# First projections of an RG-LRU layer in blocks 1 to 9: strip pairs by seven block products on half of the contraction

## The reference

```python
u = rms_norm(x, g_pre[0])
proj = u @ w_in                       # 2048 x 5120
xr, gate = proj[..., :2560], proj[..., 2560:]
xc = conv_b + sum(xpad[:, k:k + T] * conv_w[k] for k in range(4))
r = sigmoid(blockwise(xc) @ w_r + b_r); i = sigmoid(blockwise(xc) @ w_i + b_i)   # 10 blocks of 256
a = exp(-8 * r * softplus(-lam)); b = sqrt(1 - a * a) * (i * xc)
h_t = a_t * h_(t-1) + b_t
y = h * silu(gate);  out = y @ w_out
```

## Time and profile before

| | us |
|---|---|
| three runs | 1775.84, 1776.43, 1777.09; median 1776.43 |
| profiled execution | 1776.33 |
| its span, first to last instruction | 1774.6 |
| mean granted clock of TensorE | 0.990 |
| TensorE busy | 1726.0 |
| VectorE, ScalarE, GpSimd busy | 1063.4, 880.8, 234.5 |

### The profile page before, as it was taken

How to read it: one execution, slowest core, us unless ns; L and a number is a source line. 1 busy time by engine, 2 the same in 40 slices (tenths; PEclk the granted TensorE clock), 3 DMA queues, 4 the chain that set the end, 5 groups by cost and what they waited for, 6 DMA issues and landing times.

```text
span 1774.6 us, 35741 instructions
## 1 busy us (share of the span) xinstructions
PE 1726.0 (97%) x14123; PEld 1673.3 (94%) x14123; DVE 1063.4 (60%) x1781; ACT 880.8 (50%) x1385; POOL 234.5 (13%) x182
## 2 busy tenths in 40 slices
PE   8999999999999999999999999999999999899997
PEld 7999999999999999999999999999998899799995
DVE  5676555675557632358856576665665666722365
ACT  6344443344434422345566666666675666622344
POOL 2000000000000011003132222322321121001110
PEclk9999999999999999999999999999999999999997
DMA  9232223323222232665522222222224787522565
GB/s 280 87 96 81 84 84 92 97 72 94 83 84 82 75 89 80 182 175 149 187 85 61 84 61 72 73 72 60 85 60 132 228 250 234 159 84 83 153 173 185
DMA packets 311715, 205.97 MB, mean 116 GB/s; under 512 B 9041, under 2 KB 287713, under 8 KB 311521
## 3 DMA queue, kind: packets, MB, share of 16 engines
q1 hardware_dynamic: 308668, 194.86, 37.6%
q0 software_dynamic: 2864, 9.15, 1.5%
q10 hardware_dynamic: 68, 0.41, 0.1%
HBM read 188.42 MB, written 15.97 MB: 115 GB/s over the span
## 4 chain that ended last, share of the span: by engine, by line
PE 42%; DVE 5%; issue 2%; ACT 1%; DMA 1%; SPq 0%; ACTq 0%; DVEq 0%
PE PS L799 11%; PE PS L801 11%; PE PS L800 10%; PE Z L1133 2%; DVE T L2198 1%; PE Z L1143 1%; PE Z L1167 1%; PE Z L1039 1%; PE Z L1070 1%; PE Z L1317 1%; PE Z L1036 1%; PE Z L1048 1%; PE Z L1037 1%; PE Z L1072 1%; PE Z L1071 1%
## 5 line engine op out<-in xcount | busy, mean ns | idle before, releaser
L799 PE MATMUL PS<-U,WS 128*128 128x272 f32 x3680 | 1082.2, 294 | 14.6 <-issue 3.4
L801 PE MATMUL PS<-U,WS 128*128 128x272 f32 x3680 | 1067.0, 290 | 0.0
L800 PE MATMUL PS<-U,WS 128*128 128x272 f32 x3680 | 1062.7, 289 | 0.0
L799 PEld LDWEIGHTS PS<-U,WS 128*128 128x128 f32 x3680 | 696.1, 189 | 21.3 <-issue 10.2
L800 PEld LDWEIGHTS PS<-U,WS 128*128 128x128 f32 x3680 | 696.4, 189 | 1.9
L801 PEld LDWEIGHTS PS<-U,WS 128*128 128x128 f32 x3680 | 695.0, 189 | 0.0
L1864 DVE TENSOR_TENSOR WS<-raw,WS 128x1024 fp32r<-128x1024 f32 (+1 forms) x202 | 256.7, 1271 | 314.8 <-ACT WS L1346 311.8
L1346 ACT ACTIVATE WS<-raw 128x1024 fp32r<-128x1024 f32 (+1 forms) x204 | 211.5, 1037 | 460.5 <-PE PS L801 460.4
L681 POOL TENSOR_TENSOR raw<-raw,GN 128x1024 f32<-128x1024 f32 x76 | 150.2, 1976 | 522.0 <-DMA raw<-in_b_w_in_dram 448.6
L703 POOL COPY T<-T 128x544 f32<-128x544 f32 x2 | 1.7, 864 | 609.9 <-ACT T L1491 561.2
L2210 DVE TENSOR_TENSOR T<-T,Z 128x256 f32<-128x256 f32 (+1 forms) x64 | 33.2, 519 | 62.0 <-PE Z L1049 61.4
(11 more groups left out here) (298 smaller groups left out, 2156.7 us busy)
## 6 DMA issues: line engine op xcount, KB each, us to landing
raw<-in_a_w_in_dram SPq DMA_DIRECT2D x80, 512.0 KB, 3.9
raw<-in_b_w_in_dram SPq DMA_DIRECT2D x64, 512.0 KB, 4.0
raw<-in_a_w_out_dram SPq DMA_DIRECT2D x32, 512.0 KB, 3.9
KPG<-in_cache_k_dram SPq DMA_DIRECT2D x64, 256.0 KB, 3.0
raw<-in_b_w_out_dram SPq DMA_DIRECT2D x32, 512.0 KB, 4.0
VPG<-in_cache_v_dram SPq DMA_DIRECT2D x60, 256.0 KB, 3.3
T<-scratch_x SPq DMA_DIRECT2D x64, 136.0 KB, 3.5
RAW<-in_a_w_out_dram SPq DMA_DIRECT2D x12, 512.0 KB, 4.4
```

What stands on the lines that cost most here:

```text
L799: pe.matmul(psum, w_hi, x_hi, start=first, stop=False)
L800: pe.matmul(psum, w_hi, x_lo, start=False, stop=False)
L801: return pe.matmul(psum, w_lo, x_hi, start=False, stop=last)
```

## The change

In blocks 1 to 9 two strips of a kind (branch, q = 0; gate, q = 1) are now made as one pair p = 2(i - 1) + q. For K tiles 8 to 15 nothing changes but the order (`straight`, 96 matmuls). On K tiles 0 to 7 the pair is a product of 2 x 2 blocks: two strips by two groups of four K tiles (`KQ`), and these by two halves of the tokens. It is made with seven block products of 12 matmuls instead of eight, in the form of Winograd. They are numbered 1 to 7 here in the order of TensorE's queue (`two_strips`).

For that there are four sums of weight blocks per pair, made by GpSimd (`SUMS`), each with a high part by ScalarE (`sum_high`) and a low part by VectorE (`sum_low`), and four sums of token blocks, made once, in block 0, by VectorE (`token_difference`), each again with two parts (`XT` and slots of `U`). The x tiles 0 to 7 are loaded back for it (`XX`) and scaled by ScalarE. A running sum in one bank (`A_BANK`) is copied at three points by ScalarE (`keep`, into `SNAP`), and VectorE adds the copies to the other banks when strips are evicted.

Further: the first tap of the convolution and the squares of the decay go from VectorE to ScalarE (`conv_tap`, `chain_square`); only the K tiles 4 to 7 of unit m + 1 need parts of their own (`second_weights`); the gate products use other banks (`gate_bank`); Y keeps 4 tiles, is stored to DRAM per block (`y_store`) and read back in the last one (`y_back`), since the sums need its place; the block loops are unrolled on all engines; two memsets of GpSimd move behind the stage. The second load of a slot (units m + 2 and m + 3) waits for GpSimd's sums (`w_sum`), GpSimd for the first two loads and the low part of the fourth sum before.

TensorE (the order of products and waits), from the diff:

```diff
+            def two_strips(i, q):
+                m, p = pair(i, q)
+                pe.wait_ge(w_low, m + 1)
+                if q:
+                    pe.wait_ge(snap, 3 * p)
+                else:
+                    pe.wait_ge(gates_out, 4 if i == 1 else 4 * i - 2)
+                product(A_BANK, w_of(0, 0), x_of(0, 0), True, False, p_done)
...
+                product(c_bank(q, 0, 0), w_of(0, KQ), x_of(KQ, 0), True, False, unit_done)
+                pe.wait_ge(s_low, DIFFS + 4 * p + 1)
+                pe.wait_ge(strip_out, 4 * i)
+                product(c_bank(q, 1, 1), w_of(1, 0), x_of(0, 1), True, False, p_done)
+                pe.wait_ge(w_low, m + 2)
+                product(c_bank(q, 1, 0), w_of(1, KQ), xt_of(2), True, False, unit_done)
+                pe.wait_ge(s_low, DIFFS + 4 * p + 2)
+                pe.wait_ge(snap, 3 * p + 1)
+                product(A_BANK, s_of(0), xt_of(0), False, False, s_done)
+                pe.wait_ge(w_low, m + 3)
+                straight(0, q, 0, range(KQ), True, False)
+                pe.wait_ge(s_low, DIFFS + 4 * p + 3)
+                pe.wait_ge(snap, 3 * p + 2)
+                product(A_BANK, s_of(1), xt_of(1), False, True, s_done)
+                straight(0, q, 0, range(KQ, UT), False, False).then_inc(unit_done, 1)
+                pe.wait_ge(s_low, DIFFS + 4 * p + 4)
+                product(c_bank(q, 0, 1), s_of(0), x_of(KQ, 1), False, True, s_done)
+                pe.wait_ge(w_low, m + 4)
+                pe.wait_ge(p5_out, p + 1)
+                straight(1, q, 1, range(UT), False, True).then_inc(unit_done, 1)
```

GpSimd, with SP's loads:

```diff
+            for p in range(PAIRS):
+                m = 8 + 4 * p
+                if p:
+                    pool.wait_ge(s_low, DIFFS + 4 * p)
+                for slot in range(2):
+                    pool.wait_ge(unit_in[slot], 16 * (m // 2 + 1))
+                pool.tensor_tensor(SUMS[:, 0], a21, a22, ALU.add).then_inc(w_sum, 1)
+                pool.wait_ge(w_sum, DIFFS + 4 * p + 1)
+                pool.tensor_tensor(SUMS[:, 1], SUMS[:, 0], a11, ALU.subtract).then_inc(w_sum, 1)
+                pool.tensor_tensor(SUMS[:, 2], a11, a21, ALU.subtract).then_inc(w_sum, 1)
+                pool.wait_ge(w_sum, DIFFS + 4 * p + 2)
+                pool.tensor_tensor(SUMS[:, 3], a12, SUMS[:, 1], ALU.subtract).then_inc(w_sum, 1)
...
+                    for u in range(2):
+                        for s in range(2):
+                            if u:
+                                sp.wait_ge(w_sum, DIFFS + 4 * p + 4 - s)
+                            load_unit(m + 2 * u + s, s, w_in_a[:, u * UT:(u + 1) * UT, col + s * P:col + (s + 1) * P])
+                        if q == 0 and u == 0:
+                            load_gates(i, False)
```

VectorE's order in block 0 and in a pair:

```diff
+            def first_block():
+                first_strip(0)
+                branch(0, 0)
+                gate_low(0)
+                first_strip(1)
+                low(6, 0)
+                branch(0, 1)
+                decay_rates()
+                conv_low(0, 0)
+                low(7, 1)
+                conv_low(0, 1)
+                dve.wait_ge(x_high, KD + UT)
+                token_difference(0, XD0[:, 0], XX[:, 0:KQ, half(1)], XX[:, 0:KQ, half(0)])
+                token_difference(1, XD0[:, 1], XX[:, KQ:UT, half(1)], XD0[:, 0])
+                out_gate(0, 0)
+                low(8, 0)
+                token_difference(2, XD1[:, 0], XX[:, KQ:UT, half(0)], XD0[:, 1])
+                token_difference(3, XD1[:, 1], XX[:, KQ:UT, half(1)], XX[:, 0:KQ, half(1)])
...
+                out_gate(0, 1)
+                silu(0, 0)
+                second_weights(8, 0)
+                sum_low(0, 2, WSS[:, 0])
+            def two_strips(i, q, last):
+                m, p = pair(i, q)
+                if q:
+                    second_weights(m, p)
+                    sum_low(p, 2, WSS[:, 0])
+                    low(m + 2, 0)
+                    sum_low(p, 3, WSS[:, 1])
+                    second_strip(i, 0)
+                else:
+                    silu(i - 1, 1)
+                    gated_input(i - 1)
+                    low(m + 2, 0)
+                    if i == 1:
+                        sum_low(p, 3, WSS[:, 1])
+                both_sums(i, q)
+                sum_low(p, 4, WSS[:, 0])
+                if q:
+                    branch(i, 0)
+                else:
+                    one_minus_a2(i - 1)
+                low(m + 3, 1)
+                if q:
+                    branch(i, 1)
+                    conv_low(i, 0)
+                    conv_low(i, 1)
+                else:
+                    gate_low(i)
+                first_strip_low(i, q)
+                low(m + 4, 0)
+                first_strip_high(i, q)
+                if q == 0:
+                    recur(i - 1, 0)
+                    recur(i - 1, 1)
```

ScalarE's order in block 0, and behind a block the gates' sigmoids:

```diff
+            def first_block():
+                gate_high(0)
+                conv_tap(0, 0)
+                for kt in range(2):
+                    x_scaled(kt)
+                conv_high(0, 0)
+                high(6, 0, 3)
+                for kt in range(2, UT):
+                    x_scaled(kt)
+                conv_tap(0, 1)
+                conv_high(0, 1)
+                high(7, 1, 3)
...
+                second_weights(8, 0)
+                gate_sigmoid(0, 3)
+                second_sum(0)
...
+                m, p = pair(i + 1, 0)
+                second_weights(m, p)
+                act.wait_ge(y_done, i * 2)
+                gate_sigmoid(i, 0)
+                second_sum(p)
+                third_sum(p)
+                gate_sigmoid(i, 1)
+                sigmoid_gate(i, 0)
+                gate_sigmoid(i, 2)
+                gate_sigmoid(i, 3)
+                sigmoid_gate(i, 1)
+                y_store(i - 1)
```

More of the change, by code:

```diff
@@ L306, in build @@
         strip_out = sem("strip_out")
[L307 to L308 removed]
+        consts = sem("consts")
+        tap = sem("tap")
         rows_t = sem("rows_t")
@@ L883, in norm_sums, with product @@
                 ins.then_inc(ms_done, 1)
-            def block_a(i, first):
[L886 to L889, removed]
+            def product(z, w, x, first, last, done):
+                for c in range(KQ):
+                    w_hi, w_lo = w(c)
+                    x_hi_, x_lo_ = x(c)
+                    pe.matmul(z, w_hi, x_hi_, start=first and c == 0, stop=False, skip_group_check=True)
+                    pe.matmul(z, w_hi, x_lo_, start=False, stop=False, skip_group_check=True)
+                    ins = pe.matmul(z, w_lo, x_hi_, start=False, stop=last and c == KQ - 1, skip_group_check=True)
+                if done is not None:
+                    ins.then_inc(done, 1)
@@ new lines, in w_of, with s_of, x_of, xt_of @@
+            def w_of(slot, t0):
+                return lambda c: (WS[:, slot, 0, t0 + c, :], WS[:, slot, 1, t0 + c, :])
+            def s_of(slot):
+                return lambda c: (WSS[:, slot, 0, c, :], WSS[:, slot, 1, c, :])
+            def x_of(t0, h):
+                return lambda c: (U[:, t0 + c, half(h)], U[:, KD + t0 + c, half(h)])
+            def xt_of(n):
+                return lambda c: (XT[:, n, 0, c, :], XT[:, n, 1, c, :])
+            def straight(slot, q, j, tiles, new, last):
+                for c in tiles:
+                    for h in range(2):
+                        z, kt = c_bank(q, j, h), UT + c
+                        x_hi_, x_lo_ = U[:, kt, half(h)], U[:, KD + kt, half(h)]
+                        pe.matmul(z, WS[:, slot, 0, c, :], x_hi_, start=new and h == 1 and c == 0, stop=False, skip_group_check=True)
+                        pe.matmul(z, WS[:, slot, 0, c, :], x_lo_, start=False, stop=False, skip_group_check=True)
+                        ins = pe.matmul(z, WS[:, slot, 1, c, :], x_hi_, start=False, stop=last and c == UT - 1, skip_group_check=True)
+                return ins
@@ L891, in block_a @@
+            def block_a(i, first):
+                if first:
+                    for s in range(2, 4):
+                        pe.wait_ge(strip_out, s - 1)
+                        for u in range(2):
+                            unit(2 * s + u, u, s, range(u * UT, (u + 1) * UT), x_hi, x_lo, u == 0, u == 1)
+                else:
+                    two_strips(i, 0)
+                    two_strips(i, 1)
                 pe.wait_ge(gw_low, i + 1)
@@ new lines, in gate_half, with half_of, first_strip_low @@
+            def gate_half(i, j, h, c):
+                ins = V.tensor_tensor(y_tile(i, j)[:, half(h)], c, RS[:, half(h)], ALU.mult)
+                if h:
+                    ins.then_inc(strip_out, 1)
+            def half_of(i, q, j, h, c):
+                (gate_half if q else branch_half)(i, j, h, c)
+            def first_strip_low(i, q):
+                m, p = pair(i, q)
+                dve.wait_ge(unit_done, m + 3)
+                dve.wait_ge(snap, 3 * p + 1)
+                steps.done(V.tensor_tensor(SNAP[:, 0], SNAP[:, 0], c_bank(q, 0, 0), ALU.add))
```

(3 more changed lines are left out.)

481 lines of the change are left out of this document (329 added, 152 removed).

## The result

The changed kernel takes 1816.9 us (median of 4 runs, 1811.0 to 1818.0), the kernel before 1776.1 on the same chip: ratio 1.0226, 95% interval 1.0209 to 1.0244. The forecast was 1800 us, range 1777 to 1814: the direction was right, the time 17 us too low and 3 us outside the range.

What follows compares the result with a forecast made beforehand. TensorE, busy 97% of the span, was taken as the bound; -27.2 (fewer matmuls) + 36.5 (product 3) + 5.5 (smaller waits) + 9.6 (block 0) - 0.3 (next stage) = +24.1, so 1800 us, range 1777 to 1814.

Steps and rivals of the forecast that it cites:

- rival 3: New 4 us TensorE waits make matmuls run at half clock, 2 us each, nine times: 18 us, 1818 us; chance 0.08.
- 216 matmuls: TensorE, 18 pairs: seven products of 12 matmuls replace eight, at 0.1259 us per matmul: -27.2 us.
- product 3 of nine gate pairs: TensorE waits for the first sum's low part behind both recurrences on VectorE, 4.06 us per block: +36.5 us.
- gate 2, eight times: Gate 2 waits for gate 0's eviction on ScalarE, behind half conversions and table load: 0.4 in 8 blocks, 3.4 us.
- straight matmuls of block 1, product 6: Straight matmuls wait for slot 0's late second load (1.7 us), product 6 for a copy (0.4 us).
- block 0: Added x loads, token differences and low parts delay block 1's product 1 to 96.4 from 86.84: +9.6 us, bounds 4 and 13.
- just in the recurrences: Gate pair: GpSimd's four adds run from 1.3 to about 8.3 us, colliding with VectorE's recurrences; nearly all of 4.0 added.
- its signs of being wrong: A period of 52, GpSimd's adds at other times than the recurrences, or a clock below 0.98 in the stage.
- 0.4 late undisturbed: Without port collisions, product 3's low part ends at 11.0 where TensorE wants it at 10.57: 0.4 us late.
- The rule of the lock: Shared port: each GpSimd add blocks VectorE's SBUF-only instructions for its length less 0.28 us, 1.01 for 512 columns.
- The adds cost nothing: Rival 1: GpSimd's adds fall where VectorE idles or works from PSUM: -7.9 us, 1768 us; chance 0.11.
- Half of the collision: Rival 2: GpSimd's adds cost 2 us per block, 9 x 2.0 instead of 36.5: 1782 us; chance 0.12.

Runs made afterwards that it cites:

- e2: Changed kernel plus 28 useless matmuls on TensorE ahead of product 3's wait in each gate pair: 1802.5 us, ratio 1.0157 to the kernel before.
- e4: Kernel before plus four GpSimd adds of 128x512 per pair on memory of no use, in blocks 1 to 9: 1785.6 us, ratio 1.0054.
- e1: Changed kernel with GpSimd's sums cut to 2 of 128 columns per tile from the second pair on, output not the reference's: 1766.5 us, ratio 0.9954.
- e5: Changed kernel with the second recurrence later on VectorE, plus a one-column Sigmoid loading its table early in blocks 1 to 8: 1768.8 us, ratio 0.9956.
- e7: Changed kernel with block 0 alone reordered (units 6 and 7 loaded before the tokens, decay rates earlier): 1810.6 us, ratio 1.0197.
- e3: Changed kernel with the second recurrence moved on VectorE behind the low parts that product 3 and the straight matmuls need: 1776.5 us, ratio 1.0006.
- e8: Changed kernel plus 12 useless matmuls on TensorE ahead of the first-sum wait in each block's second pair: 1813.1 us, ratio 1.0205.

## Why the prediction was right and wrong

**The step that failed is "rival 3, the clock falls", which the forecast had at 0.08 and left out of the sum.** The sum kept the clock at 1.00 behind waits of 4 us because it had stayed 1.00 through the 3 us before the next stage. It fell during or behind all nine waits and behind the one of block 1's first product: 18.2 us measured by the matmuls' distances, where that rival priced 18 and came to 1818 us. e2 shows it as cause and, roughly, in size: same waits, TensorE not idle, 14.4 us less, with the first of the ten falls still in it. The Trainium skill's rule that an idle TensorE goes to half its clock (TensorE: Matmul & The Clock Gate, Part 1) spoke for this rival, and the trace agrees with it: 0.227 instead of 0.126 us from matmul to matmul. I gave it too little, resting on one stretch of before with 3 us of waits in two parts. The same trace of before has the opposite case 250 us later, a wait of 2.0 us and the clock at half just behind it, in the view by stretch:
```profile
832.00:834.20 2.20, 0.36 (x4) 0.14 (x2) 2.20 (x3) 0.89 (x3) 0.98 (x1) 1.00 0.00 0
834.20:838.60 4.40, 4.40 (x22) 4.32 (x23) 4.33 (x9) 2.07 (x5) 0.00 (x0) 0.61 0.02 5
```
The page's slices of 44 us show 9 there, since 3.4 us at half clock take only 0.04 from a slice's mean. So rival 3 could have been priced from a row of before.

The other terms, from the start distances of the changed kernel's matmuls, up to the first gate matmul of block 9 (614.06, and 570.44 before: +43.6):

| term | forecast | measured |
|---|---|---|
| 216 matmuls | -27.2 | -27.2 |
| product 3 of nine gate pairs | +36.5 | +35.0 |
| gate 2, eight times | +3.4 | +6.5 |
| straight matmuls of block 1, product 6 | +2.1 | +1.9 |
| block 0 | +9.6 | +7.7 |
| half clock | 0 | +18.2 |
| sum | +24.4 | +42.1 |

The last 1.5 us are the restarts: at full clock the second matmul behind a wait starts 0.23 us behind the first (244.68 to 244.91) instead of 0.126, and there are 18 waits. (At half clock it is 0.39, and what is over 0.23 stands in the clock's term.) The next stage's start gave 0.3 back, as forecast. Later stages, with the same instructions, were 4 us shorter in this profiled execution, with 5 us in one stretch:
```profile
1356.30:1602.20 245.90, 236.43 (x2703) 220.39 (x2702) 159.93 (x253) 151.03 (x230) 37.52 (x19) 0.99 0.62 187
```
The same stretch of before, and its mean clock:
```profile
1312.00:1563.00 251.00, 239.48 (x2702) 223.02 (x2701) 162.94 (x253) 151.13 (x230) 37.07 (x19) 0.98 0.62 184
```
e4, which leaves those stages alone, shows the same there (11.1 us behind at 703 us, 9.0 at 1600), so this is no effect of the change. Part of it is the clock again: in these stretches it is at half for 3.4 us three times in the kernel before (from 1350, 1364 and 1552 us) and once in the changed one (from 1588), and TensorE's busy time is 3.0 us less. The rest is shorter waits; why they differ stays open.

**Product 3** was right in size, 3.89 us a block for 4.06, and only partly in place. The forecast put the sums "just in the recurrences"; that the sums fall elsewhere was another of its signs of being wrong. They started when the load was forecast to land (231.57 is 1.2 us behind the end of the straight matmuls, forecast 1.3), but three of the four met the low part and the strip's second half that the forecast's own times put there, and only the last a recurrence. It didn't matter, since all of it is ahead of L2326 in the same queue. "0.4 late undisturbed" was too high: 3.74 measured less 3.88 of collisions is -0.1, and e1 shows no wait. (By the forecast's own terms, 0.4 and 4.04, it would have been 4.4 a block and not the 4.06 that stands in its sum.) The forecast also took the strips' evictions for PSUM work, which the port leaves alone; here they add into SNAP first, and what follows (L2274) reads two SBUF inputs and is held up.

**The rule of the lock.** The forecast took 1.01 us per sum from the earlier trace rows; measured are 1.06, 0.63, 1.09 and 1.10. By the whole length that the Trainium skill gives (SBUF — State Buffer, SBUF: two separate sides), it would have been 4 x 1.29 = 5.2 us, an estimate; the trace has 3.88. Most of that distance isn't the rule's: VectorE's instructions started 0.1 to 1.4 us behind the sum that they met, and counted from their own start to the end of the sum's row they would have lost 1.19, 0.76, 1.22 and 1.24, 4.4 us in all. Each went on 0.13 us before that end. The 0.14 us that the forecast took off at the start of an add as well were only VectorE's later start (934.49 against 934.36); no row shows them as part of the lock.

**Gate 2** was mis-sized: it waits 0.81 us, not 0.4. e5 shows that the table load is the whole of it. **Block 0** was right in kind (product 1 at 94.5, forecast 96.4). The 7.7 us of the table hold a gain that isn't block 0's: up to 73 us, where the matmuls and their order are those of before, the changed kernel's trace is 0.75 us ahead (the same matmul starts at 51.60 and at 52.36). Traces differ there by up to 2.8 us, and block 0's own price is 8.5 us. In e7 that matmul starts at 52.12 and product 1 at 87.6, a price of 1.1, so block 0's order, not its work, holds most of it; but the straight matmuls of block 1 then wait 3.8 us instead of 1.4, and two of e7's nine waits for the sum are not followed by slow matmuls, so its 6.3 us are not block 0's alone.

**The rivals.** "The adds cost nothing", 1768 us, is what e1 measures with the sums' work taken away (1766.5), and what the order of e3 comes near to. Nothing in the case speaks for it in the order that the change has. Half of the collision, 1782 us, is out too: all four sums cost VectorE time, and all of it reached product 3.

## What to carry to other kernels

An operation given to an idle GpSimd is paid on VectorE when both read two SBUF inputs: count its length on both, and look for what stands behind it in VectorE's queue and has a due time. Here moving one recurrence past the urgent half split was worth 40 us, the whole algorithm change 27. When TensorE gets a new wait of over 2 us, price the matmuls behind it at half clock for some 3 to 5 us as well, and count a table load among the costs of the first Sigmoid after another function.

## What the runs showed of the hardware

- At a wait of 3.7 us or more the granted clock of TensorE falls to half either 1.1 to 1.5 us behind the restart (from 0.1 us on in e7), for 15 to 16 matmuls of 272 columns at 0.227 us instead of 0.126 (six of ten falls in the changed kernel, 1.5 us each), or during the wait, and then 20 to 23 matmuls are slow from the first one on (four of ten, 2.0 to 2.4 us each). Waits of 0.8 us were never followed by it, that of 2.0 us at 832 in the kernel before was, those of 2.3 us were in six of eight cases (e8), those of 3.7 us in all nine of the changed kernel and in seven of nine in e7. What decides between two equal waits stays open; the length of the pause alone does not.
- The lock between GpSimd and VectorE doesn't depend on size: a copy of 24 columns (L2275) stood still for 1.09 us beside a sum.
- The other way round GpSimd stretched as well: the second sum took 2.15 us instead of 1.28, as the low part on VectorE (L2178) that it met had its turn in between.
